# The mixer stage of a hybrid S5, retention and convolution decoder: another order of its branches, other layouts of its states, another engine for one addition and another queue for one store

## The reference, cut to what matters

```
u = rmsnorm(h);  z = u @ w_in
s5_out,  s5 states   = s5_branch(...)         # scan, Re(C h) + D u, GLU
ret_out, ret_state   = retention_branch(...)  # 4 heads, 128 x 256 state for each head and sample
conv_out, conv_state = conv_branch(...)       # GLU, causal depthwise conv of width 31, norm, swish
gates  = sigmoid(z[..., OFF_GATE:])           # three gates of 1024 channels
merged = gates[0] * (s5_out @ s5_proj) + gates[1] * (ret_out @ ret_proj) + gates[2] * (conv_out @ conv_proj)
h = h + merged @ w_out
h = h + ffn(rmsnorm(h))                       # layer 0: dense; layer 1: 2 of 8 experts
```

## Time and profile before

| | us |
|---|---|
| median of 3 runs | 1994.8 (1992.23 to 1999.01) |
| the profiled execution | 1989.37 |
| its span, first to last instruction | 1987.6 |
| PE busy in the span | 1862.7 (94%) |
| DVE busy | 1556.9 (78%) |
| ACT busy | 1197.2 (60%) |
| POOL busy | 366.5 (18%) |

### The profile page before, as it was taken

How to read it: one execution, slowest core, us unless ns; L and a number is a source line. 1 busy time by engine, 2 the same in 40 slices (tenths; PEclk the granted TensorE clock), 3 DMA queues, 4 the chain that set the end, 5 groups by cost and what they waited for, 6 DMA issues and landing times.

```text
span 1987.6 us, 31588 instructions
## 1 busy us (share of the span) xinstructions
PE 1862.7 (94%) x11792; PEld 1579.8 (79%) x11792; DVE 1556.9 (78%) x1767; ACT 1197.2 (60%) x1277; POOL 366.5 (18%) x469
## 2 busy tenths in 40 slices
PE   7877899999998986999999999999999999999995
PEld 6866699999998974999777777777777777777773
DVE  6987696556746965867588888888888888889885
ACT  4343455454434362555567777777676777777765
POOL 7986100059900043000000000000000000000000
PEclk8998899999999997999799999999999999999998
DMA  5546654555555639345599999999999999999996
GB/s 192 174 124 175 132 186 159 170 162 182 180 192 164 196 107 210 128 168 181 214 361 365 383 356 364 374 361 385 351 375 371 367 382 352 380 361 375 375 355 225
DMA packets 107107, 527.52 MB, mean 265 GB/s; under 512 B 22103, under 2 KB 23607, under 8 KB 63063
## 3 DMA queue, kind: packets, MB, share of 16 engines
q1 hardware_dynamic: 96727, 489.80, 67.2%
q0 software_dynamic: 9232, 35.35, 7.5%
q10 hardware_dynamic: 1056, 1.08, 0.2%
HBM read 505.69 MB, written 20.50 MB: 265 GB/s over the span
## 4 chain that ended last, share of the span: by engine, by line
PE 75%; POOL 8%; DVE 5%; DMA 4%; issue 4%; ACT 4%; DVEq 0%; ACTq 0%; POOLq 0%; SPq 0%
PE bank L641 23%; PE bank L643 23%; PE bank L642 23%; POOL s5m L2021 3%; DVE s5m_parts L1937 2%; POOL work L2021 1%; DMA out_ret_s<-zone 1%; PE bank L1013 1%; DMA zone<-in_sret 1%; DMA out_ret_s<-work 1%; PE bank L674 1%; ACT zone_parts L1378 1%; PE bank L967 1%; DVE ring_parts L1437 1%; POOL sq L2006 1%
## 5 line engine op out<-in xcount | busy, mean ns | idle before, releaser
L1937 DVE TENSOR_TENSOR s5m_parts<-s5m,ring_parts 128x2048 fp32r<-128x2048 f32 x228 | 519.4, 2287 | 78.7 <-ACT ring_parts L1378 78.1
L1378 ACT ACTIVATE ring_parts<-s5m 128x2048 fp32r<-128x2048 f32 x228 | 431.9, 1917 | 87.7 <-DMA s5m<-in_experts 84.4
L1437 DVE TENSOR_TENSOR ring_parts<-ring,ring_parts 128x1024 fp32r<-128x1024 f32 x238 | 314.3, 1325 | 199.3 <-ACT ring_parts L1072 167.6
L641 PE MATMUL bank<-uT_parts,ring_parts 128*128 128x264 f32 x1312 | 384.2, 293 | 25.3 <-DVE uT_parts L1454 16.2
L642 PE MATMUL bank<-uT_hi,ring_parts 128*128 128x264 f32 x1312 | 378.8, 289 | 0.0
L643 PE MATMUL bank<-uT_hi,ring_parts 128*128 128x264 f32 x1312 | 377.7, 288 | 0.0
L641 PE MATMUL bank<-s5m_parts,work_parts 128*112 128x512 f32 x896 | 359.2, 401 | 1.1 <-DVE table_parts L1929 1.1
L1072 ACT ACTIVATE ring_parts<-ring 128x1024 fp32r<-128x1024 f32 x238 | 251.1, 1056 | 158.4 <-PE bank L643 131.0
L1937 DVE TENSOR_TENSOR s5m_parts<-s5m,zone_parts 128x2048 fp32r<-128x2048 f32 x112 | 255.9, 2289 | 52.9 <-ACT zone_parts L1378 52.7
L641 PEld LDWEIGHTS bank<-uT_parts,ring_parts 128*128 128x128 f32 x1312 | 254.0, 194 | 32.8 <-issue 31.4
L642 PEld LDWEIGHTS bank<-uT_hi,ring_parts 128*128 128x128 f32 x1312 | 254.6, 194 | 0.1
(11 more groups left out here) (330 smaller groups left out, 3065.3 us busy)
## 6 DMA issues: line engine op xcount, KB each, us to landing
s5m<-in_experts SPq DMA_DIRECT2D x340, 1024.0 KB, 6.6
ring<-in_weights SPq DMA_DIRECT2D x238, 512.0 KB, 3.3
work<-in_sret POOLq DMA_DIRECT2D x8, 512.0 KB, 7.1
zone<-in_sret POOLq DMA_DIRECT2D x8, 512.0 KB, 8.5
out_ret_s<-work POOLq DMA_DIRECT2D x8, 512.0 KB, 8.5
s5m<-kscr POOLq DMA_DIRECT2D x16, 256.0 KB, 9.9
out_ret_s<-zone POOLq DMA_DIRECT2D x8, 512.0 KB, 9.2
xT<-in_xT SPq DMA_DIRECT2D x1, 1056.0 KB, 5.5
```

The lines of the kernel that those rows point to most:

```text
L641: pe.matmul(out, left[0], right[1], start=first, stop=False)
L1378: act.activation(high_slot(c), slot(c, s5m), ACT.Copy).then_inc(high_done, 1)
L1437: dve.tensor_tensor(weights(c, ring_parts), weights(c, ring), f32(weights_hi(c)), ALU.subtract).then_inc(low_done, 1)
L1937: dve.tensor_tensor(slot(c, s5m_parts), slot(c, s5m), f32(high_slot(c)), ALU.subtract).then_inc(low_done, 1)
```

## The change

- The S5 branch goes in front of the retention's: `gs`, `gl`, `ps` come before `gr`, `pr`. Two `gg` tiles go in front of `win`. The samples no longer stand one behind each `gg`: sample 0 stands behind `si`, 1 to 3 behind `gg` 3, 4 and 6, then `y`, then 4 behind `gs` 0, 5 behind `gl`, 6 and 7 among the `ps`.
- States in long runs: `sret`, `ret_s`, `ret_p`, `convst`, `conv_s`, `h0` are laid out in DRAM so that each partition's part is one run (4 KB for a retention state, four runs of 1 KB before).
- The direct term is multiplied out early on POOL and added by DVE. The store of `kk` and its eight loads are started by SP, one behind the other, after the load of the sixth chunk behind `gg` 1's; SP stands still there for `kmat_ready` and for the store.
- The variance of all heads is one tile `gv` with a head in every 32 partitions and one reciprocal; four matmuls `rb` spread it again. The multiplication by `silu(g)` comes first.
- `phases` goes behind the tiles `zs`, `CONV_AT` gets other numbers, and buffers move into `s5m`.

The diff's core:

```diff
-CONV_AT = {"zs": (2, 4), "v": (2, 3), "pre": (0, 4), "ret": (3, 2), "si": (16, 12), "os": (2, 1), "gr": (6, 6),
-           "gs": (3, 2)}
+CONV_AT = {"zs": (2, 4), "v": (2, 3), "pre": (0, 4), "ret": (3, 2), "si": (16, 12), "os": (2, 2), "y": (4, 4),
+           "gs": (4, 4), "gr": (11, 8)}
...
+SAMPLE_BEHIND = {3: 1, 4: 2, 6: 3}
...
         add("vs", 2); add("ks", 1)
+        add("gg", 2, KD)
         add("win", 8)
         add("kk", 2)
         add("si", 4)
-        for b in range(NS):
-            o += [((l, "gg", b), KD)]
-            if b > 0:
-                o += [((l, "os", b - 1), 0)]
-            o += [((l, "oa", b), 0), ((l, "ob", b), 0)]
-        o += [((l, "os", NS - 1), 0), ((l, "gr", 0), KD), ((l, "ot", 0), 0)]
-        add("gm", 4); add("gv", 4)
+        o += sample(l, 0)
+        for d in range(2, KD):
+            o += [((l, "gg", d), KD)]
+            if d in SAMPLE_BEHIND:
+                o += sample(l, SAMPLE_BEHIND[d])
         add("y", 4)
-        o += [((l, "gr", 1), KD)]
+        o += [((l, "gs", 0), KD)] + sample(l, 4)
         add("yt", 4)
...
+                    if n == CHUNK_OF[(l, "gg", 1)] + RING:
+
+                        before = (S - 1) * G * GP
+                        sp.wait_ge(kmat_ready, l + 1)
+                        sp.dma_start(kscr[:, before:before + S * G * GP], s5m[0:GP, 0:S * G * GP]).then_inc(kscr_out, 16)
+                        sp.wait_ge(kscr_out, 16 * (l + 1))
...
+                        for s in range(S):
+                            lo = (S - 1 - s) * G * GP
+                            sp.dma_start(s5m[s * GP:(s + 1) * GP, 0:S * G * GP], kscr[:, lo:lo + S * G * GP]).then_inc(toep_in, 16)
...
+                dve.wait_ge(dd_ready, l + 1)
+                add(toep[0:GP, 0, :, :], toep[0:GP, 0, :, :], dd).then_inc(kmat_ready, 1)
...
+                sample_update(0)
+                conv_ops(l, "os")
+                sweep(l, 2)
+                sample_update(1)
+                conv_ops(l, "os")
+                sweep(l, 3)
+                sample_update(2)
+                sweep(l, 4)
+                sweep(l, 5)
+                sample_update(3)
                 sweep(l, 6)
...
-    f["sret"] = x["state_ret"]
+    f["sret"] = x["state_ret"].transpose(0, 1, 3, 2, 4)
```

More of the change, by code:

```diff
@@ L112, in tile_order @@
             o += [((l, "pr", d), KD)]
[L113 to L116, removed]
+            if d == 4:
                 add("cm", 1)
@@ L787, in _ @@
                 mm.then_inc(mm_done, 1)
+                for d in range(2):
+                    weight_tile((l, "gg", d), "u", KD)
                 pe.wait_ge(gb_ready, l + 1)
@@ L839, in _, with sample_step @@
                     pe.wait_ge(*out_of(key))
-                for b in range(NS):
-                    weight_tile((l, "gg", b), "u", KD)
+                def sample_step(b):
                     if b > 0:
@@ L1166, in _, with gate_out @@
                 last.then_inc(stack_high, 1)
+                def gate_out(d):
+                    key = (l, "gg", d)
+                    full(key)
+                    act.activation(mT[:, d, :], at(key)[:, 0:T], ACT.Silu).then_inc(freed(key), 1)
+                for key in ((l, "vs", 0), (l, "vs", 1), (l, "ks", 0)):
+                    evicted_by_dve(key)
+                for d in range(2):
+                    gate_out(d)
                 for i in range(8):
@@ L1193, in _ @@
                 masked(1)
-                for b in range(NS):
-                    key = (l, "gg", b)
-                    full(key)
-                    act.activation(mT[:, b, :], at(key)[:, 0:T], ACT.Silu).then_inc(freed(key), 1)
-                    if b + 2 < NS:
-                        masked(b + 2)
+                masked(2)
+                for d in range(2, KD):
+                    gate_out(d)
+                    if d in SAMPLE_BEHIND:
+                        masked(SAMPLE_BEHIND[d] + 2)
                 def gate_of(name, d, of):
@@ L1321, in _ @@
                         high((l, "n", d), uT[:, d, :])
+                    for b in range(2, 4):
+                        act.wait_ge(s_out[b], 32 * (l + 1))
                     for f in range(F_DENSE):
@@ L1612, in _ @@
                     conv_ops(l, "zs")
+                if l == 0:
+                    phases()
                 dve.wait_ge(table_in, 16 * (2 * l + 1))
@@ new lines, in _ @@
+                conv_ops(l, "y")
+                low_weights(CHUNK_OF[(l, "gs", 0)] + 2)
+                sample_update(4)
+                for m in range(4):
+                    low((l, "y", m), yg[:, m, :])
+                for m in range(4):
+                    evicted_by_act((l, "gl", m))
+                    mul(glu[:, m, :], yg[:, m, :], glu[:, m, :]).then_inc(glu_done, 1)
+                    if m >= 2:
+                        low((l, "g", m - 2), glu[:, m - 2, :])
+                for m in (2, 3):
+                    low((l, "g", m), glu[:, m, :])
```

400 lines of the change are left out of this document (219 added, 181 removed).

## The result

The changed kernel takes 1970.97 us (median of 4 runs, 1968.71 to 1975.0), the kernel before, run beside it, 1993.51 (4 runs, 1990.23 to 1999.01): a ratio of 0.9878, interval 0.9852 to 0.9903. The gain is 22.5 us by the medians and 17.9 by the spans of the profiled executions (1987.6 and 1969.7). Faster, as forecast, and inside the range; but 31.8 were forecast, so 9.3 us of it are missing by the medians and 13.9 by the spans.

A forecast was written before the change was run, and what follows sets the result against it. PE's waits for state updates, with half-clock matmuls behind them, lost 67.0 us. Gains of 16.1 (layer 0) and 18.5 (layer 1), less 2.8 for the clock, made 31.8, forecasting 1963 us; its own range 1953 to 1973, overall 1944 to 1987.

The forecast's parts named there:

- The waits for the updated states: Mixer: PE's `os` waits for DVE's update of a sample's state, 44.2 us over both layers, would go.
- sample 0: PE in front of sample 0, behind `si`: a stall of 3.0 us in each layer.
- first `pr`: First four pairs of chunks: DVE, with convolution, needs longer than PE; 5.0 us lost in layer 0, 1.2 in layer 1.
- DVE's chain: DVE's work from `kk` to `h_ready`: 29.5 us, ending at t + 46.6, where t is the end of `ks`.
- the rival of a chain made dear by POOL: POOL's `turns` slow DVE's whole chain by 1.45, 13 us more a layer, 1989 us; chance 0.07 in full.
- phases: Layer 0, small DVE operations moved to where DVE is full: cost 4.4 us, bounds 0 and 4.5.
- up to `y`: PE's stalls behind `gg` 4 and 6 and at `y`: 5.6 us a layer.
- `rb`: PE at `rb` waits for one reciprocal, 1.81, and a multiplication of 0.4: 2.3 us a layer.
- sums of `gv`, `rb`: PE's column sums and broadcasts for means and variances: unchanged at 7.8 us, bounds -2 and +2 a layer.
- the half clock: PE's clock falls behind stalls of 2 to 3 us: 0.7 each, two a layer, 2.8 us in all.
- Reloads: Eight loads of `kk` on SP: 10 to 13 us, landed by t + 36, 10 ahead of `y`, costing nothing.
- The sign listed under "wrong": PE or ACT waiting for the weights of `gg` 7 would show the forecast wrong; no size given.

The follow-up runs named there:

- e3: The changed kernel with the samples' retention states in DRAM laid out as before, four runs of 1 KB per partition: 1972.94 us.
- e4: The kernel before with only the samples' retention states put in long runs, one of 4 KB per partition: 1989.82 us.
- e6: The changed kernel with one load of 128 partitions in place of the eight reloads of `kk`, same bytes, S5 output changed: 1966.95 us.
- e1: The changed kernel with `phases` back at its old place, ahead of the convolution's operations of `si`: 1965.12 us.
- e11: The changed kernel with POOL holding back the first updated state's output until the eight reloads have landed: 1970.25 us.
- e2: The changed kernel with the store of `kk` and its eight reloads started by POOL behind its `turns`, not by SP: 1979.19 us.

## Why the prediction was right, and where its sum failed

**Right: where the time was.** The waits for the updated states went altogether, and not by the layout (e3, e4) but by the order: samples 4 to 7 come behind `y` and their states' transfers have the time. Sample 0 waits 2.91 and 2.55 (forecast 3.0), the first `pr` of layer 0 and their `gr` 0.56 + 0.78 + 3.18 = 4.5 (5.0, though in four even parts). DVE's chain without late weights ends at t + 46.3 (e6), forecast t + 46.6, so the rival of a chain made dear by POOL is out.

**The terms of the sum**, us lost in layer 0 / layer 1:

| term | forecast | measured | |
|---|---|---|---|
| phases | 4.4 / 0 | 10.4 / 0 | shift of t against the earlier trace rows; e1 |
| sample 0 | 3.0 / 3.0 | 2.9 / 2.6 | its error is inside the next row |
| up to `y` | 5.6 / 5.6 | 9.8 / 7.3 | `y` at t + 50.8 / t + 48.3, t + 41 in the forecast without a wait |
| `rb` | 2.3 / 2.3 | 3.8 / 3.8 | |
| first `pr` | 5.0 / 1.2 | 4.5 / 2.4 | |
| sums of `gv`, `rb` | 0 / 0 | -2.2 / -2.2 | 5.6 in place of 7.8, just past the bound of -2 |
| `gc` 1 | 0 / 0 | 0.7 / 0.7 | waits 1.74, and 1.05 in the kernel before |

The row up to `y` is reckoned as in the forecast, with sample 0 inside the 41. Measured less forecast is 6.0 + 5.9 + 3.0 + 0.7 - 4.4 + 1.4 = 12.6 of the 13.9 between 31.8 and the 17.9 of the spans. The other 1.3 have no row; the 2.8 us for the half clock are left as forecast, though part of it lies in the row up to `y`. That the time stayed inside 1953 to 1973 is partly luck: four terms were too small, and the sums, put at nothing, gave 4.4 back.

**Phases: the step that failed.** The term of 4.4, with its bounds of 0 and 4.5, took the operations' duration from a place where POOL stood still. At the new place POOL works, and they took 13.07. The bound was no bound. The window of the kernel before from 62 to 76 us (first line) could have told it; the second is the changed kernel:

```profile
62.00:76.00 14.00, 12.20 (x96) 11.60 (x95) 13.80 (x19) 5.00 (x5) 13.84 (x15) 1.00 0.56 189
62.00:76.00 14.00, 2.33 (x20) 2.12 (x18) 13.35 (x23) 1.65 (x2) 13.77 (x22) 0.68 0.29 100
```

POOL was busy for 13.84 of the 14 us, which makes the operations dear, and DVE for 13.80, which leaves them nowhere to hide; PE had 12.20 there and has 2.33 now. Taking them out of the later chain was worth less than that: to put them back gains 5.9 by the medians (e1).

**Reloads: mis-sized, and what stood behind them left out.** The prediction took 10 to 13 us for them, to t + 36, and put their cost at nothing. They took 18.5, to t + 39.6 (185.87), and the weights of `gg` 7, whose place on PE was free at 186.95, came after them, at 189.23. The reloads themselves were in time for `y`, 11 us ahead of it (10 in the forecast); the weights behind them were not, and as their low parts stand inside DVE's chain they moved `h_ready` from t + 46.3 to t + 50.0, which is nearly all that the row up to `y` has over its forecast. The sign listed under "wrong", PE or ACT waiting for the weights of `gg` 7, is what the trace shows. The rule of the Trainium skill, "SBUF — State Buffer", section "Can I just issue two DMAs to hit both halves?", that such transfers serialize, holds: one every 2.1 us in e11. Its 104 GB/s for 16 partitions (section "Door 1: The DMA port swizzle") gave the estimate of 20 us in all, against 125 GB/s and 16.8 here: nearer than the 10 to 13. The price of it is what e6 gives back, 4.0 us by the medians.

**`rb`: a term too small.** The forecast counted one reciprocal of 1.81 and "a multiplication of 0.4 in front of it", 2.3 in all; it was 3.84 because a chunk's low part of 1.22 stood in front of both on DVE (263.12, 264.26 and the reciprocal 1.80 at 264.60). An instruction already in the program has to be counted with the wait.

**Open.** `gc` 1 waits 1.74 for a low part in all of these kernels: in the trace of layer 0 DVE idles 6.63 us in front of it, for ACT, which rounds that chunk only at 329.10, behind a table load of 1.28 us and the convolution's own operations. To move it was not tried. Nor was it tried to keep POOL out of the stretch of the phases instead of moving them.

## What to carry to other kernels

Before work is moved into a stretch of an engine, price it there, beside what the other engines do in it, not where it came from. When a queue gets transfers that fill only some partitions, ask how long they hold up the other transfers, which weights come behind, and what stands behind those weights on the engine that works them up, and not only when they land themselves. And when a large wait has been taken away, go through the small ones that are left: three edits, two of order and one of a table, were worth almost as much (19.3 us) as the whole change (22.5).

## What the runs showed of the hardware

- **Small operations of DVE beside POOL.** 128x32 operations took 0.56 to 0.75 us while POOL started an operation every 0.60 to 0.69, each ending 0.04 to 0.05 us behind one of POOL's, and 0.18 to 0.19 where it stood still (e1). Here it hits operations with all operands in SBUF; those that read PSUM (`bank`) are not slower. The groups of DVE by line from 60 to 80 us of the changed kernel (mean ns behind the busy time):

```profile
L1522 DVE TENSOR_TENSOR lw<-lw 128x32 f32<-128x32 f32 x13 | 8.1, 628 | 0.4
...
L1629 DVE SCALAR_TENSOR_TENSOR zone<-zone,vecs 128x256 f32<-128x256 f32 x2 | 1.7, 867 | 0.0
L1695 DVE SCALAR_TENSOR_TENSOR tmp<-bank,table 64x264 f32<-64x264 f32 (+1 forms) x3 | 1.3, 427 | 0.0
```

  The convolution's 128x256 took 867 ns there and 480 ns from 280 to 284 us, where POOL did nothing; the one that reads `bank` 427 ns, and 0.42 to 0.44 us elsewhere with POOL or without. Not all operations in SBUF are hit: `TENSOR_REDUCE` of the samples' convolution took 0.41 us in both cases. The Trainium skill, "GPSIMD Engine Reference", section "Key points", says that the two engines share SBUF interfaces and collide where a DVE instruction has two SBUF inputs or runs in what it calls a 2-port mode. The trace agrees for the two-input operations of this stretch. The single-input operation on `lw` at 71.39 also took 0.63 us (0.18 in e1), and in which mode it ran no run shows. That a small operation waits for one of POOL's to end is read from the common ends; POOL was never slowed or stopped at that place to test it.
- **Loads into 16 partitions hold up what is started behind them.** Eight of 256 KB went at 125 GB/s in a row, and weights of 512 KB that were started behind them took 12 to 15 us by the medians, from the same queue (e11) or from another (e2), in place of 3.9; they moved at 414 GB/s as soon as the eight were done (e11).
